# Two token tiles on four fixed experts instead of two experts at a time, with finer weight refills and a reordered last unit

## The chip, the cores and the metric

The kernel runs on one core of a Trainium2 chip. The metric is the device time of one execution in microseconds, lower is better; the core's span (first to last instruction) is inside it.

## What is computed

One transformer layer on 256 tokens of 1024 float32 values: a mixer (global and windowed attention, whose output projection is added to `h`), then a hierarchical mixture of experts, then a final RMSNorm. The part that matters here:

```
gl = xt @ w_group + b_group             # 4 groups, the best one is taken
el = xt @ w_expert + b_expert           # 8 experts per group, the best two are taken
h_e = silu(xt @ w_gate[e]) * (xt @ w_up[e])          # 1024 -> 512
y  += combine[:, e] * (h_e @ w_down[e])              # 512 -> 1024
out = rms_norm(h + y, final_g)
```

There are 32 experts of three 2 MB float32 matrices each, 201 MB in all, and every expert's weights are read from DRAM once.

## The kernel before

The 256 tokens are two tiles (`TT = 2`) of 128. Tokens of an expert are gathered into columns by a matmul with a 0/1 matrix (`pick`), run through gate, up and down, and scattered back to their rows by a matmul with the transposed weighted picks (`place_w`), summing in four PSUM banks Y0 to Y3.

**Units.** The 32 experts are worked in ten units (`WAYS`, line 45): a 2-way unit takes two experts of 64 columns, a 4-way unit four of 32. The columns of TensorE's array are split between them, so two matmuls of 64 columns, or four of 32, run side by side. Experts 0 to 3 are fixed in advance (units 0 and 1); the rest are sorted on the chip by token count, the four fullest of them in the 2-way units 4 and 5.

**Weights.** All weights go through a ring of 12 slots of 2 MB. Fill `f` of the ring (`fill_at`, unit, matrix, expert) is in slot `f % 12`. SyncE (SP) issues every load in order and waits, before each, until the last user of the slot is done (L345, and L374 to L389 for unit 2). The 12 slots take the four fixed experts before the routing is known; from there on a slot can be refilled only when (a) the order of the experts has been computed (`order_ready`, then `value_load` of each expert's number, L374) and (b) TensorE has done with what is in it. Unit 2's loads are the first that need both. Unit 2's gate matrices come in pieces as unit 0's gate product goes (`GATE_PIECES`, `load_chunks`, L389): 256 KB, 256 KB, then 512 KB each, for two experts; the rest of unit 2's 12 fills comes in halves of 1 MB (`load_piece`, L381).

**The order around the routing, written out by hand, per engine.** TensorE (PE): transposes `h` (`turn_h`, L1239), the last of the eight output projections (`project(0, 1, 1, 0)`, L1333), router logits of tile 0 and of tile 1 (`router_logits`, L1426), then rank and count matmuls (L1454 to L1466), gathers for unit 0 (`first_gather`, L1449), one matmul that turns the sort into expert numbers (L1593), and unit 0's gate product (L1584). VectorE (DVE): adds the projection (`add_projection`, L870), tile 0's routing chain (L976 to L1007: best group, best two experts, `chosen`), the same for tile 1, picks of unit 0 (`first_pick`, L1016), the sort (L1109 to L1122) interleaved with the combine weights (L1112 to L1138), the cast of the expert numbers (L1131), and the picks of the next units (L1068, L1077). ScalarE (ACT): squares for the second norm (L694, L701), copies of the transposes (L697, L703), gathered activations (L714), silu (L724), `y` copies (`copy_out`, L728).

**Steady state.** For each later unit: gather, transpose of the previous unit's activations (`turn_act`, L1525), down product (L1536), gate product (L1511), scatter (L1566), transposed picks (L1490), up product (L1511).

**The last unit.** Its down matrices arrive in five column pieces (`LAST_PIECES`, L449). After the up product PE runs the spread of the final gain over the partitions (`spread_final_g`, L1665, two halves, on either side of `turn_act`), the first half of down (`last_half`, L1536), then scatter and two quarters of down in turn (`last_quarter` L1684, `last_scatter` L1696), each scatter behind an ACT copy of what it scatters (`last_copy`, L738). ACT squares the sums (L745), DVE and GpSimd make the norm factor (L1220, L1212, L571), DVE and ACT scale, and the stores go out.

```
last_half(); last_scatter(0)
last_quarter(0, range(FC)); last_scatter(1)
last_quarter(1, ...);       last_scatter(2)
```

## Time and profile before

| | |
|---|---|
| three runs | 551.67 us median (551.37 to 551.74) |
| the profiled execution | 551.39 us |
| its span | 549.3 us |
| mean granted TensorE clock | 0.910 |
| TensorE busy | 445.6 us (81%) |
| VectorE, ScalarE, GpSimd busy | 108.3, 81.0, 28.4 us |
| SyncE's DMA queue | 214.89 MB, 94.2% of 16 engines' span |
| chain that ended last | PE 48%, DMA 47% of the span |

Times are microseconds from the first instruction. In the rows, PE is TensorE's matmul, PEld its weight load, DVE VectorE, ACT ScalarE, SPq SyncE's instructions that issue DMAs. L12 is line 12 of the kernel. "x4" is a count, and `[2.29 <-DMA ...]` the idle time of the engine just before, with what ended it.

### The profile page before, as it was taken

Reading aid. Unit: us, or ns where it says so; the run is one execution under the profiler, and the core shown is the slowest. Engines: PE = TensorE matmul, PEld = TensorE weight load, DVE = VectorE, ACT = ScalarE, POOL = GpSimd, SP = SyncE. Lnnn points to the kernel's source line nnn. Section 1 sums busy time; section 2 is a strip of 40 time slices with the busy share of each in tenths; the row PEclk is TensorE's granted clock in tenths of the full one; section 3 lists DMA queues with packets and bytes.
Section 4 is the critical chain, followed back from the end, with each engine's and each line's share of the span. In section 5 each row is a group of like instructions: output and inputs, shape, how many; then the busy total and the mean of one; then the engine's idle time right before and its main releaser. Section 6 shows DMA issues by size and latency. Waiting matters only on the chain.

```text
span 549.3 us, 6418 instructions
## 1 busy us (share of the span) xinstructions
PE 445.6 (81%) x2528; PEld 193.6 (35%) x2528; DVE 108.3 (20%) x352; ACT 81.0 (15%) x218; POOL 28.4 (5%) x61
## 2 busy tenths in 40 slices
PE   9999999999999985759999984863686295657794
PEld 4455554664453431323532521410223021312232
DVE  1028863251150300210200400400031000300012
ACT  1127653311100101000101001000100000000113
POOL 0242422100000000000000000000000000000000
PEclk9999999999999999779999988975878787977898
DMA  8989996959999999999999999999999999999992
GB/s 307 367 322 424 432 404 227 366 199 376 425 421 420 430 428 428 424 430 425 427 430 428 427 426 430 427 430 426 427 428 428 426 430 425 432 424 431 419 378 102
DMA packets 27822, 217.72 MB, mean 396 GB/s; under 512 B 5352, under 2 KB 7784, under 8 KB 14480
## 3 DMA queue, kind: packets, MB, share of 16 engines
q1 hardware_dynamic: 23552, 214.89, 94.2%
q10 hardware_dynamic: 4240, 2.42, 1.5%
q8 instruction: 21, 0.34, 0.3%
q14 instruction: 9, 0.07, 0.0%
HBM read 216.23 MB, written 1.06 MB: 396 GB/s over the span
## 4 chain that ended last, share of the span: by engine, by line
PE 48%; DMA 47%; another core or an unknown queue 1%; SPq 1%; issue 1%; DVE 1%; ACT 0%; DVEq 0%; POOL 0%
DMA ring<-in_w_up_dram 26%; DMA ring<-in_w_gate_dram 21%; PE bank L1511 18%; PE bank L1245 8%; PE bank L1333 5%; PE bank L1536 3%; PE bank L1287 2%; PE bank L1311 1%; PE bank L1299 1%; PE bank L1472 1%; PE bank L1566 1%; PE bank L1584 1%; SPq L345 1%; PE bank L1449 1%
## 5 line engine op out<-in xcount | busy, mean ns | idle before, releaser
L1511 PE MATMUL bank<-ring,head 128*32 128x512 f32 (+1 forms) x992 | 155.0, 676 | 69.3 <-DMA ring<-in_w_gate_dram 36.6
L1511 PEld LDWEIGHTS bank<-ring,head 128*32 128x32 f32 (+1 forms) x992 | 44.8, 128 | 170.1 <-issue 169.9
L1536 PE MATMUL bank<-ring,region_q 128*32 128x512 f32 (+1 forms) x480 | 75.8, 671 | 23.8 <-DMA ring<-in_w_down_dram 22.9
L1106 DVE COPY region_q<-bank 128x256 f32<-128x256 f32 x10 | 4.2, 424 | 300.8 <-PE bank L1490 300.8
L1536 PEld LDWEIGHTS bank<-ring,region_q 128*32 128x32 f32 (+1 forms) x480 | 22.3, 129 | 69.9 <-issue 69.3
L728 ACT ACTIVATE head<-bank 128x512 f32<-128x512 f32 x18 | 9.9, 595 | 234.7 <-PE bank L1566 228.1
L1245 PE MATMUL bank<-ring,head 128*128 128x512 f32 x96 | 44.4, 612 | 0.0
L1472 PEld LDWEIGHTS bank<-region_q,h 128*128 128x128 f32 x288 | 33.7, 192 | 8.2 <-issue 8.2
L1472 PE MATMUL bank<-region_q,h 128*128 128x128 f32 x288 | 36.3, 279 | 0.0
L1566 PE MATMUL bank<-head,region_q 128*128 128x512 f32 x72 | 33.3, 605 | 1.2 <-ACT head L728 1.2
L714 ACT ACTIVATE head<-bank,head 128x128 f32<-128x128 f32 x40 | 11.4, 369 | 121.4 <-PE bank L1472 119.9
L1245 PEld LDWEIGHTS bank<-ring,head 128*128 128x128 f32 x96 | 18.0, 196 | 21.4 <-issue 20.9
L571 POOL TENSOR_TENSOR stat<-stat 128x1 f32<-128x1 f32 x2 | 1.1, 550 | 434.7 <-DVE stat L1212 434.7
L1566 PEld LDWEIGHTS bank<-head,region_q 128*128 128x128 f32 x72 | 12.9, 189 | 21.6 <-issue 19.6
L1333 PE MATMUL bank<-ring,head 128*128 128x512 f32 x32 | 15.1, 598 | 0.0
L1333 PE MATMUL bank<-ring,region_q 128*128 128x512 f32 x32 | 14.7, 601 | 0.0
L1068 DVE TENSOR_SCALAR region_q<-cst,sorted_rw,stat 128x32 f32<-128x32 f32 (+1 forms) x56 | 12.4, 296 | 0.0
L1077 DVE TENSOR_SCALAR region_q<-cst,sorted_rw 128x32 f32<-128x32 f32 (+1 forms) x56 | 12.4, 295 | 0.0
L1095 DVE COPY region_q<-bank 128x512 f32<-128x512 f32 x10 | 6.9, 692 | 16.0 <-PE bank L1525 16.0
L1100 DVE TENSOR_TENSOR region_q<-region_q,bank 128x512 f32<-128x512 f32 x10 | 6.9, 687 | 16.1 <-PE bank L1511 16.1
L1090 DVE TENSOR_TENSOR head<-bank,head 128x512 f32<-128x512 f32 x9 | 6.2, 692 | 17.1 <-PE bank L1472 17.1
L870 DVE SCALAR_TENSOR_TENSOR h<-bank,stat,h 128x512 f32<-128x512 f32 x8 | 6.0, 751 | 16.4 <-PE bank L1333 9.8
(199 smaller groups left out, 310.9 us busy)
## 6 DMA issues: line engine op xcount, KB each, us to landing
ring<-in_w_gate_dram SPq DMA_DIRECT2D x28, 2048.0 KB, 39.5
ring<-in_w_up_dram SPq DMA_DIRECT2D x28, 2048.0 KB, 38.8
ring<-in_w_down_dram SPq DMA_DIRECT2D x24, 2048.0 KB, 39.2
ring<-in_w_down_dram SPq DMA_DIRECT2D x12, 1024.0 KB, 12.1
ring<-in_w_up_dram SPq DMA_DIRECT2D x8, 1024.0 KB, 10.0
ring<-in_w_o_dram SPq DMA_DIRECT2D x2, 2048.0 KB, 13.1
ring<-in_w_gate_dram SPq DMA_DIRECT2D x4, 1024.0 KB, 9.8
ring<-in_w_in_dram SPq DMA_DIRECT2D x7, 512.0 KB, 8.8
```

The source lines that it names most:

```text
L714: last = act.activation(xgT[:, c, :], ps[GD0 if i else FIRST_BANKS[c // 2]][:, c * P:(c + 1) * P], ACT.Copy, scale=g2_rows[:, c:c + 1])
L728: act.activation(y_slots[:, 512 * half:512 * half + 512], ps[(GD0 if i else Y0) + half][:], ACT.Copy).then_inc(y_ready, 1)
L1068: last = dve.tensor_scalar(pick[:, t, rows * a:rows * (a + 1)], iota1[:, 0:rows], ranks[:, t, e0 + a:e0 + a + 1], rstd2[:, t:t + 1], ALU.i ...
L1077: last = dve.tensor_scalar(pick_w[:, t, rows * a:rows * (a + 1)], iota1[:, 0:rows], ranks[:, t, e0 + a:e0 + a + 1], weights[:, t, e0 + a:e ...
L1095: dve.tensor_copy(hT, ps[GATE][:].rearrange("p (c s) -> p c s", c=FC)).then_inc(hT_ready, 1)
L1245: return pe.matmul(ps[bank][:], xT[:, c, t * P:(t + 1) * P], cols, start=(c == 0), stop=(c == KC - 1))
L1287: last = pe.matmul(ps[2 * (s % 2) + half][:, 256 * j:256 * j + 256], qkT[rows, 5 * g + 2 * jg + j, qt * P:(qt + 1) * P], qkT[rows, 5 * g + ...
L1333: last = pe.matmul(ps[bank][:], mixT[g][:, t, c, :], w_o_sb[g][:, c, 512 * half:512 * half + 512], start=(c == 0), stop=(c == 3))
L1472: last = pe.matmul(ps[GD0 + b][:, c * P:(c + 1) * P], h_cols[:, t, 4 * b + c, :], pick[:, t, :], start=(t == 0), stop=(t == TT - 1))
L1511: last = pe.matmul(ps[bank][rows, :], xgT[:, c, rows], slots[fill_slot(f + a)][:, c * F:(c + 1) * F], start=(c == 0), stop=(c == KC - 1))
L1536: last = pe.matmul(ps[bank + half][rows, :], hT[:, c, rows], down_cols(slots[fill_slot(f + a)], half, c), start=(c == 0), stop=(c == FC - 1))
L1566: last = pe.matmul(ps[Y0 + k][:], place_w[i % 2][:, (k // 2) * P:(k // 2 + 1) * P], y_slots[:, 512 * (k % 2):512 * (k % 2) + 512], start=( ...
```

## The change

Units 0 and 1 now hold one token tile each and both work with the same four fixed experts at 32 columns. The same 12 fills are loaded before the routing is known, and the same loads wait for the same steps of the attention (only the matrices that they carry differ). What changes:

- Tile 0 is picked, gathered and put through its first gate chunk before tile 1 has been routed. For that the last projection is split around tile 0's router logits, its addition on DVE is put into tile 0's routing chain, the squares for tile 1's norm are taken in two halves, and each tile has its own picks (`first_picks`, four instructions instead of two).
- The sort and the cast of the expert numbers stand ahead of the combine weights on DVE. On PE the expert-number matmul stands behind tile 0's whole gather and half of tile 1's.
- Each chunk of the fixed experts' weights is used for tile 0, then for tile 1, and is then free. Unit 2's gate matrices come in 16 loads of 256 KB and 8 of 512 KB, its up matrices in 8 of 512 KB and 4 of 1 MB, its down matrices in 8 of 1 MB.
- For a fixed expert the check on capacity uses the fuller of the two tiles against 32.
- `spread_final_g` moves ahead of the last unit's up product. The second quarter of the last down product follows the first without a scatter between, the scatter of the first quarter is split into its two tiles around the last chunk, and the last copy is made by DVE instead of ACT, before DVE's branch on the overflow flag. The final product of the first 512 columns is put ahead of that branch too.

```diff
-GATE_PIECES = ((0, 1), (1, 2), (2, 4), (4, 6), (6, 8))
+GATE_PIECES = ((0, 1), (1, 2), (2, 3), (3, 4), (4, 6), (6, 8))
+UP_PIECES = ((0, 2), (2, 4), (4, 8))
-WAYS = (2, 2, 4, 4, 2, 2, 4, 4, 4, 4)
+WAYS = (FIXED, FIXED, 4, 4, 2, 2, 4, 4, 4, 4)
...
SyncE, unit 2
             experts = order_of(2, range(2))
-            for k in range(PIECES):
...
+            for k, (lo, hi) in enumerate(GATE_PIECES):
+                if hi < KC:
                     sp.wait_ge(gate_pieces, k + 1)
                 else:
+                    sp.wait_ge(gate_done, 2)
+                for a in range(FIXED):
+                    if k == 0 and a >= 2:
+                        experts += order_of(2, range(a, a + 1))
+                    load_chunks(0, a, lo, hi, gate_pieces_in)
+            for k, (lo, hi) in enumerate(UP_PIECES):
...
+                for a in range(FIXED):
+                    load_chunks(1, a, lo, hi, up_pieces_in)
+            for half in range(2):
+                sp.wait_ge(down_done, 3 + half)
+                for a in range(FIXED):
+                    load_chunks(2, a, 4 * half, 4 * half + 4, down_half_in)
...
VectorE, routing
-            after(best_experts(0))
+            k_best = best_experts(0)
+            add_projection(0, 1, 1, 8, 0)
+            after(k_best)
             after(expert_places(0))
             link(two_hots(0))
             choose(0)
+            dve.wait_ge(chosen_ready, 1)
+            dve.tensor_copy(chosen_late[:, FIXED:EXPERTS], chosen[:, 0, FIXED:EXPERTS]).then_inc(chosen_ready, 1)
+            first_picks(0)
+            rank_tile(0)
...
-            dve.wait_ge(ranked, 2)
-            first_pick(1, 0)
-            first_pick(1, 1).then_inc(pick_ready, 1)
-            rank_tile(1)
+            first_picks(1)
+            k_rank = rank_tile(1)
...
TensorE, routing
             turn_h(0, 0)
             turn_h(0, 1)
-            project(0, 1, 1, 0)
-            turn_h(1, 0)
+            project(0, 1, 1, 0, range(0, 2))
             pe.wait_ge(hTr_act, 2)
             pe.wait_ge(router_ready, 1)
             router_logits(0, range(KC)).then_inc(routed, 1)
+            project(0, 1, 1, 0, range(2, 4))
+            turn_h(1, 0)
             turn_h(1, 1)
             pe.wait_ge(hTr_act, 3)
             router_logits(1, range(0, 4))
+            pe.wait_ge(chosen_ready, 1)
+            pe.matmul(ps[RANK0][:, 0:EXPERTS], upper_low, chosen[:, 0, :], start=True, stop=True).then_inc(ranked, 1)
             pe.wait_ge(hTr_act, 4)
             router_logits(1, range(4, 8)).then_inc(routed, 1)
...
+            pe.wait_ge(pick_ready, 1)
+            tile_gather(0, range(0, 4))
+            tile_gather(0, range(4, KC))
             pe.wait_ge(hots_ready, 1)
...
+            tile_products(0, 0, range(0, 1))
+            pe.wait_ge(pick_ready, 2)
+            tile_gather(1, range(0, 2))
+            tile_gather(1, range(2, 4))
+            pe.wait_ge(places_ready, 1)
+            pe.matmul(ps[ORDER][0:1, 128:128 + EXPERTS], expert_col, place_hot[0:EXPERTS], start=True, stop=True).then_inc(ordered, 1)
+            tile_products(1, 0, range(0, 1)).then_inc(gate_pieces, 1)
+            both_tiles(0, range(1, 2))
+            pe.wait_ge(xg_act, 1)
+            tile_gather(1, range(4, KC))
+            for lo, hi in GATE_PIECES[2:]:
+                both_tiles(0, range(lo, hi))
...
TensorE, last unit
                 if i == UNITS - 1:
                     scatter(i - 1)
+                    spread_final_g(0, GD0)
+                    spread_final_g(1, GD1)
...
-            spread_final_g(0, GD0)
             turn_act(UNITS - 1)
-            spread_final_g(1, UP)
...
             last_quarter(0, range(FC))
-            last_scatter(1)
             pe.wait_ge(last_in[2], 16 * 4)
-            pe.wait_ge(y_ready, 2 * (UNITS - 1) + 2)
             last_quarter(1, range(0, 2))
             pe.wait_ge(last_in[3], 16 * 4)
             last_quarter(1, range(2, 3))
+            last_scatter(1, range(0, 1))
             pe.wait_ge(last_in[4], 16 * 4)
             last_quarter(1, range(3, 4))
+            last_scatter(1, range(1, 2))
             last_scatter(2)
```

The new helpers: `tile_gather(t, chunks)` is one 128x128 matmul per chunk of tile `t`; `tile_products(t, m, chunks)` is four matmuls of 32 columns per chunk; `both_tiles` runs it for tile 0, then tile 1, and signals SyncE; `tile_down(t)` is `down` for one tile.

## Rows read from the trace of the kernel before

**Rows 1.** The page's slices: GB/s in 40 equal slices of the span.
```profile
GB/s 307 367 322 424 432 404 227 366 199 376 425 421 420 430 428 428 424 430 425 427 430 428 427 426 430 427 430 426 427 428 428 426 430 425 432 424 431 419 378 102
```

**Rows 2.** Windows: from:to and length, busy by engine, clock, DMA share, GB/s.
```profile
170.00:530.00 360.00, 266.63 (x1658) 102.54 (x1658) 39.06 (x127) 21.47 (x54) 0.00 (x0) 0.87 1.01 427
117.00:142.00 25.00, 25.00 (x138) 11.54 (x134) 4.01 (x12) 3.03 (x8) 0.00 (x0) 1.00 0.95 353
117.00:118.00 1.00, 1.00 (x8) 0.42 (x6) 0.00 (x0) 0.10 (x1) 0.00 (x0) 1.00 0.02 6
118.00:122.00 4.00, 4.00 (x24) 2.04 (x22) 2.03 (x8) 0.00 (x0) 0.00 (x0) 1.00 0.90 262
122.00:126.00 4.00, 4.00 (x22) 1.38 (x20) 0.60 (x3) 0.60 (x1) 0.00 (x0) 1.00 1.01 377
```

**Rows 3.** SyncE's waits from 100 to 180 us: total, times, longest.
```profile
SPq L374 <- DVE stat L1133: 9.7, 1, 9.7
```

**Rows 4.** Timeline, the routing up to the first refill: start, duration, instruction.
```profile
102.02 3.60 PE L1333 MATMUL bank<-ring,region_q 128*128 128x512 f32 x8
105.66 0.75 DVE L870 SCALAR_TENSOR_TENSOR h<-bank,stat,h 128x512 f32<-128x512 f32 x1 [3.56 <-PE bank L1333]
105.89 1.95 PE L1426 MATMUL bank<-region_q,head 128*128 128x128 f32 x16
107.98 0.22 DVE L976 SCALAR_TENSOR_TENSOR region_q<-bank,stat,router_b 128x4 f32<-128x4 f32 x1 [1.55 <-PE bank L1426]
...
109.98 0.19 DVE L1007 TENSOR_TENSOR region_q<-region_q 128x32 f32<-128x32 f32 x1
...
113.46 1.60 PE L1449 MATMUL bank<-region_q,h 128*128 128x128 f32 x12
...
114.99 0.21 PE L1593 MATMUL bank<-stat,cst 32*1 32x32 f32 x2
115.24 0.18 DVE L1131 CAST expert_at<-bank 1x32 int32<-1x32 f32 x1 [0.15 <-PE bank L1593]
116.96 0.36 SPq L389 DMA_DIRECT2D ring<-in_w_gate_dram  x1
```

**Rows 5.** Timeline, a later set of 32-column picks on VectorE.
```profile
152.06 1.75 DVE L1068 TENSOR_SCALAR region_q<-cst,sorted_rw,stat 128x32 f32<-128x32 f32 x8
```

**Rows 6.** DMA issues by size (us from issue to landing), four issues in a row, expert-number loads.
```profile
ring<-in_w_gate_dram SPq DMA_DIRECT2D x4, 256.0 KB, 3.4
```
```profile
178.42 1.89 SPq L345 DMA_DIRECT2D ring<-in_w_gate_dram  x4
```
```profile
L374 SPq TENSOR_LOAD <-expert_at x28: 260/266/468, 115.5 to 436.9; - x28
```

**Rows 7.** Timeline of TensorE from the last up product on.
```profile
517.90 5.34 PE L1511 MATMUL bank<-ring,head 128*32 128x512 f32 x32 [2.29 <-DMA ring<-in_w_up_dram]
...
523.53 3.64 PE L1511 MATMUL bank<-ring,head 128*32 128x512 f32 x32
527.10 1.16 PE L1665 MATMUL bank<-cst,head 128*128 128x128 f32 x8
...
535.90 1.93 PE L1684 MATMUL bank<-ring,region_q 128*32 128x256 f32 x32
538.34 1.13 PE L1696 MATMUL bank<-head,region_q 128*128 128x256 f32 x4 [0.50 <-ACT head L738]
...
541.83 1.13 PE L1696 MATMUL bank<-head,region_q 128*128 128x256 f32 x4 [0.50 <-ACT head L738]
```

**Rows 8.** TensorE's waits from 480 us on: total, times, longest.
```profile
PE bank L1511 <- DMA ring<-in_w_up_dram: 2.3, 1, 2.3
PE bank L1696 <- ACT head L738: 1.7, 3, 0.7
PE bank L1566 <- ACT head L728: 1.2, 1, 1.2
```

**Rows 9.** Windows around the last up product: columns as in rows 2.
```profile
516.00:518.00 2.00, 0.10 (x4) 0.13 (x8) 0.00 (x0) 0.00 (x0) 0.00 (x0) 1.00 1.00 418
520.00:522.00 2.00, 2.00 (x12) 0.54 (x8) 0.00 (x0) 0.00 (x0) 0.00 (x0) 0.50 1.03 422
```

More of the change, by code:

```diff
@@ L1499, in landed, with products @@
                 pe.wait_ge(slot_in[fill_slot(f)], 16 * fill_count(f))
-            def products(i, n_e, f, bank, done, pieces=None, every=2, picks=False, chunks=range(KC)):
+            def products(i, n_e, f, bank, done, picks=False):
                 pe.wait_ge(xg_act, i + 1)
@@ L1564, in scatter @@
                 pe.wait_ge(place_ready, i + 1)
-                for k in range(4):
-                    last = pe.matmul(ps[Y0 + k][:], place_w[i % 2][:, (k // 2) * P:(k // 2 + 1) * P],
-                                     y_slots[:, 512 * (k % 2):512 * (k % 2) + 512], start=(i == 0), stop=False)
-                    last.then_inc(scattered, 1)
+                for t in tiles(i):
+                    for half in range(2):
+                        last = pe.matmul(ps[Y0 + 2 * t + half][:], place_w[i % 2][:, t * P:(t + 1) * P],
+                                         y_slots[:, 512 * half:512 * half + 512], start=(i < ONE_TILE), stop=False)
+                        last.then_inc(scattered, TT // len(tiles(i)))
                 return last
@@ L1744, in _ @@
                             for c in range(FC):
[L1745 removed]
+                                last = pe.matmul(ps[3 + half][:], hT[:, c, :], down_cols(slots[OVER_SLOT + 2], half, c),
                                                  start=(c == 0), stop=(c == FC - 1))
```

536 lines of the change are left out of this document (248 added, 288 removed).

## The prediction, made before the changed kernel was run

> **What bounds the kernel now.** I read the slices first: the core moves 420 to 432 GB/s in nearly every slice from 137 us (slice 11) to 508 us, and falls to 199 to 376 GB/s in slices 7 to 10 [rows 1]. The windows then put numbers on it: 427 GB/s and a DMA share of 1.01 from 170 to 530 us, while TensorE is busy for 267 of those 360 us [rows 2]. So in this stretch the weight stream is the bound and TensorE has slack. 32 experts of weights must pass whatever the order of work, and the change keeps their bytes. It can gain or lose at two places only: when and how fast the stream restarts behind the routing, and how long the chain is from the last up weights to the end.
>
> The restart: SyncE sits 9.7 us in one wait, for DVE's order of the experts [rows 3]. The chain behind it is PE's expert-number matmul at 114.99, the cast at 115.24, the first refill at 116.96 [rows 4]. The end: PE waits 2.29 us for the last up weights until 517.90, then works without a DMA wait to the last scatter at 541.83 [rows 7, 8].
>
> The sum is made against the profiled execution, 551.39 us with a span of 549.3; the median of the runs stands 0.28 us above it.
>
> **Part 1, TensorE's work on the fixed experts.** Before: two units of 24 chunk groups, two matmuls side by side in each. After: two tiles of 24 groups, four side by side. Thirty-two matmuls of that form (8 groups) took 3.64 us [rows 7], 0.455 us a group, so 48 groups are about 22 us either way. Scatters and gathers of the two units halve. Price zero: the cover is the stream, which needs 25 MB / 427 GB/s, some 59 us, for the 12 slots that this work frees. All 16.8 MB of gate and up fills are freed by about 138 us by this count, the down slots some 10 us later, and the stream reaches them only at 118.7 + 16.8 MB / 0.427 = 158 us. If the cover were gone, a late `turn_act` (DVE makes unit 2's picks before the product of tile 0, about 4 us) would be paid.
>
> **Part 2, when the order is known.** I move each step in the timeline.
> - Tile 0. Half the projection (1.80 of 3.60 us), then the logits (1.95) [rows 4]: logits done at 105.8, 2.1 us earlier than now. DVE's chain starts at 105.9. `add_projection` now stands inside it and waits for the projection's second half (to 107.5); it takes 0.75, so the chain's 2.19 us (from L976 at 107.98 to the end of L1007 at 110.17) [rows 4] becomes 3.2: `chosen` at 109.1, 1.1 us earlier.
> - Tile 1. `h` is complete at 108.3 instead of 106.4. Transposes, ACT's copy behind the second half of the square, and eight chunks of logits with the rank matmul between end at 111.2 instead of 110.1. DVE meanwhile makes four picks of tile 0; eight of them take 1.75 us, so 0.22 each [rows 5], 0.9 in all, then the rank. Its second chain starts at 111.4 and gives the two hots at 113.4, about 1 us later than now.
> - PE is behind by then: tile 0's whole gather is 16 instructions. Twelve take 1.60 us [rows 4], so 2.1 us, from 111.8 to 113.9. Then the ranks, DVE's four picks of tile 1 (0.9) at 114.6 to 115.5, its rank, the sort (0.9, ending 116.4). On PE half of tile 1's gather (1.1) runs beside it, to 116.7.
> - So the expert-number matmul stands at about 116.7, not 114.99: **+1.7 us**. The load of the numbers and the first issue follow as now. Tile 1's first gate chunk is done by about 117.5, before SyncE needs it at 118.7. The last fixed fill (down, 2 MB) is issued 1.9 us later with `projected`, at 107.5, and ends near 114.6, still before the restart. Bounds of this term: +0.4 (DVE's picks and PE's gather all hidden, only the 1 us of tile 1 minus what the sort gains by standing alone) to +3.0 (my chain plus one more round trip between the engines at each of the five handovers).
>
> **Part 3, how fast the stream fills after the restart.** Before: 353 GB/s from 117 to 142 is 8.8 MB, which at 427 takes 20.7 us, so 4.3 us are lost here. Nearly 1 us of it is the start (6 GB/s from 117 to 118), then 262 GB/s while the 256 KB pieces run, 377 while 512 KB ones do [rows 2]. After: 16 pieces of 256 KB instead of 4. SyncE issues one each 0.52 us (four issues in 1.89, less 0.33 for the last, by three) [rows 6], except in the first round, where a number is loaded ahead of the third and fourth, 0.27 us for the load instruction alone [rows 6] and about 0.55 with its checks. A 256 KB piece moves in 0.61 us at 427 GB/s, so after the first four the queue gets deep, as it never was before. I take 0.95 us for the start, 262 GB/s for the first MB (4.0 us), and 350 GB/s for the other 3.1 MB, between the 377 of the half-MB pieces and the 262: 9.0 us. That is 13.9 us for 4.2 MB, against 9.8 at full rate, 4.1 lost. The 16 loads of 512 KB (8.4 MB) are taken close to the full rate with a deep queue, 0.3 lost. Sum 4.4 against 4.3: **+0.1 us**. Bounds: -2.1 (start, and 377 GB/s for all of the 4.2 MB) and +5.4 (262 for the 4.2 MB, 6.2 lost, and 377 for the 8.4 MB, 2.6 lost, with the start 9.7 to 9.8).
>
> A rule speaks against this step. The Trainium skill, "DMA: Bandwidth & Descriptors", section Bandwidth, says to batch transfers to 1 MiB or more for 75% of peak, and lists 341 GB/s for 1 MB alone. The trace half agrees: four 256 KB pieces ran at 262 GB/s; but half-MB ones in a queue ran at 377, above that table's 1 MB.
>
> **Part 4, the last unit.** The scatters wait for ACT's copies three times, 1.7 us in all, the first 0.7, the other two 0.5 each [rows 8]. Both 0.5 go: the first quarter's copy runs beside the second quarter (1.93) and the last copy, now on DVE, beside half a scatter (0.57 of 1.13) [rows 7]. Two scatter halves lengthened by a wait for the square of tile 1 give about 0.15 back: **-0.85 us**. DVE's branch on the flag moves to before the norm factor; I cost it at nothing, covered by the last scatter and squares. Bounds -1.0 to 0 (branch and copy not covered, or the last weights land too late: they must land by about 539).
>
> The spread (1.16 + about 1.1 us) [rows 7] was hidden beside DVE's product and copy; moving it away saves nothing there. But it now fills the 2.29 us in which PE waits for the up weights. The window 516:518 shows PE busy for 0.10 of 2 us at full clock, then 520:522 shows the clock granted at 0.50, the 1.2 GHz level [rows 9], and the first half of the up product takes 5.34 us where the second takes 3.64 [rows 7]. With the spread in that gap I expect full clock: **-1.7 us**, bounds -1.7 and 0.
>
> **The sum:** 551.39 + 1.7 + 0.1 - 0.85 - 1.7 = 550.64, plus 0.28 for the median: 550.9 us. About 0.2% (1.1 us) is what a measurement of this kernel can tell from no change, so the likeliest case counts as the same, close to its edge.
>
> **Rivals.**
> - *The clock falls all the same.* PE still has the 1.2 us wait for ACT's `y` copies before the last scatter of the steady state [rows 8]. Then 552.6, at the upper edge of no change. For it: the granted clock averages 0.87 from 170 to 530 us [rows 2], so it falls often. Against: the gap is nearly gone. Chance 0.22, split about evenly between same and slower.
> - *Small refills run slowly.* Place: SyncE's queue from 118.7 us on. Price +5.4 instead of +0.1: 556.2. It decides from the point where the first 4.2 MB run below about 280 GB/s (15.9 us with the start instead of 13.9), which brings the sum over 552.8. For it: 262 GB/s is the only measured rate of 256 KB pieces. Against: in that window only four such pieces were to be had, with SyncE waiting for TensorE. Chance 0.12, slower.
> - *The order is known no later.* If the sort without interleaved work and tile 0's early start make up for the picks, the +1.7 is 0.4 or less: 549.6, faster. For it: tile 0 is 1.1 us earlier. Against: the order needs tile 1, and tile 1's `h` comes 1.9 us later. Chance 0.22.
> - *The change does nothing measurable.* Restart as now, tail bound by the last weights: 551.7. Chance 0.06.
>
> The forecast has the remaining 0.38, its own range 549.8 to 552.2, of which 0.12 lie below 550.6. So faster 0.12 + 0.22 = 0.34, slower 0.11 + 0.12 = 0.23 and with the forecast's far end 0.25, same 0.41. The range that leaves out 2 in 10: 549.2 (under it the case of an early restart with a fast refill, 0.1) to 554.0 (above it the slow refills, 0.1).
>
> **What would show it.** The expert-number matmul near 116.7 and the first refill near 118.7 (part 2); a window of 25 us from the first refill on at about 350 GB/s (part 3); from 170 us on 427 GB/s as now (part 1; if PE's late work starved the stream, the rate would dip between 140 and 165 us); the last up product in about 7.4 us instead of 9.2, and one ACT wait before L1696's successors instead of three (part 4). I am wrong if the first refill starts before 117.5 or after 120, or if the last up product's first half keeps 5.3 us.

## The result, and the profile of the changed kernel

The changed kernel takes **553.74 us** (median of 7 runs) beside 551.37 for the kernel before on the same chip (7 runs, 549.65 to 552.3): ratio **1.0047**, 95% interval [1.0031, 1.0063], so 1.7 to 3.5 us slower. The forecast was 550.9. One execution of the changed kernel took 1478.22 us; no run of this study explains it, and the interval leaves it out (the median of the other six is 553.51). The profiled execution took 552.5 us, its span is 550.6.

The page's slices, in GB/s of 40 equal slices, answer to [rows 1]:

```profile
GB/s 317 359 329 426 429 405 233 315 202 354 404 387 420 429 427 427 427 430 427 426 430 423 432 424 430 425 431 426 428 427 427 428 427 427 427 427 430 420 405 150
```

Slices 10 to 13 are what to look at (slice 1 is the first). The kernel before reached 425 in slice 11 and kept it; here it is 404, then 387, and 420 only from slice 13 on. The windows (columns as in [rows 2]) put the loss into stretches. First the changed kernel, then two stretches of the kernel before that were not shown yet:

```profile
117.00:142.00 25.00, 25.00 (x228) 8.86 (x224) 6.49 (x31) 1.97 (x3) 0.00 (x0) 1.00 0.91 315
118.00:120.00 2.00, 2.00 (x20) 1.13 (x16) 0.19 (x1) 0.00 (x0) 0.00 (x0) 1.00 0.57 150
120.00:124.00 4.00, 4.00 (x44) 1.22 (x40) 2.56 (x12) 0.00 (x0) 0.00 (x0) 1.00 0.88 262
124.00:128.00 4.00, 4.00 (x44) 1.25 (x40) 0.00 (x0) 0.00 (x0) 0.00 (x0) 1.00 0.94 262
160.00:168.00 8.00, 8.00 (x80) 2.85 (x73) 0.00 (x0) 0.00 (x0) 0.00 (x0) 1.00 0.91 356
170.00:530.00 360.00, 258.01 (x1606) 99.59 (x1598) 38.36 (x126) 21.78 (x54) 0.00 (x0) 0.86 1.01 427
```
```profile
118.00:142.00 24.00, 24.00 (x132) 11.11 (x128) 4.01 (x12) 2.94 (x7) 0.00 (x0) 1.00 0.99 367
160.00:168.00 8.00, 7.12 (x47) 4.67 (x48) 1.38 (x2) 1.14 (x4) 0.00 (x0) 1.00 1.02 422
```

From 170 us on both run at 427 GB/s, so a byte that is late at 170 stays late. The yardstick of this study is therefore the **loss** of a stretch: its length times (1 - rate / 427). From 118 to 142 us it is 3.4 us before and 5.6 after, from 142 to 160 it is 0.2 and 0.5, from 160 to 168 it is 0.1 and 1.3. The sum is 3.7 us before and 7.4 after, **3.7 us more**. The last up weights show the same: they let TensorE start at 521.31 instead of 517.90.

SyncE's waits (100 to 180 us; total, times, longest), answering to [rows 3], name who holds the refills back, and the timeline answers to [rows 4] for the restart:

```profile
SPq L395 <- PE bank L1559: 15.1, 2, 13.8
SPq L395 <- PE bank L1532: 9.4, 3, 6.7
SPq L389 <- DVE stat L1123: 9.1, 1, 9.1
```
```profile
101.42 1.88 PE L1335 MATMUL bank<-ring,region_q 128*128 128x512 f32 x4
105.22 0.22 DVE L975 SCALAR_TENSOR_TENSOR region_q<-bank,stat,router_b 128x4 f32<-128x4 f32 x1 [3.57 <-PE bank L1428]
108.06 0.19 DVE L1006 TENSOR_TENSOR region_q<-region_q 128x32 f32<-128x32 f32 x1
110.44 0.22 DVE L975 SCALAR_TENSOR_TENSOR region_q<-bank,stat,router_b 128x4 f32<-128x4 f32 x1
113.18 0.94 DVE L1017 TENSOR_SCALAR region_q<-cst,bank,stat 128x32 f32<-128x32 f32 x4 [0.40 <-PE bank L1463]
115.69 0.21 PE L1630 MATMUL bank<-stat,cst 32*1 32x32 f32 x2
116.01 0.18 DVE L1122 CAST expert_at<-bank 1x32 int32<-1x32 f32 x1 [0.88 <-PE bank L1630]
117.71 0.36 SPq L395 DMA_DIRECT2D ring<-in_w_gate_dram  x1
```

The first refill is at 117.71 instead of 116.96, but this execution reached the last projection 0.6 us earlier (101.42, first line, against 102.02 in [rows 4]). Counted from the start of that projection the first refill stands at 14.94 us in all six profiles that keep the code before up to there. It stands at 16.29 to 16.31 in nine of the eleven with the changed routing, and at 15.88 in a_order_first and a_both, which move the expert-number matmul forward. So the changed kernel's first refill comes **1.35 us later**.

Counted in the same way, the loss is 4.3 us more, the 3.7 of above and the 0.6 by which this execution was ahead. It can be read from windows of 51 us that begin 15 us behind the start of that projection. Before, then after:

```profile
117.02:168.02 51.00, 50.12 (x275) 23.52 (x273) 13.17 (x45) 5.34 (x14) 0.00 (x0) 1.00 0.98 388
116.42:167.42 51.00, 49.88 (x452) 19.70 (x444) 12.41 (x50) 5.47 (x11) 0.00 (x0) 1.00 0.94 352
```

That is 4.7 us lost against 9.0. These 51 us hold the later start, the slower restart and the dry stretch together, and a profile gives them more surely than a part of them: 386 to 389 GB/s in the six profiles that keep the code before, 351 to 355 in the nine of the changed kernel and its variants that leave no work out.

Next, TensorE's work on the fixed experts, and SyncE at the down refills:

```profile
139.21 5.36 PE L1532 MATMUL bank<-ring,head 128*32 128x512 f32 x48
147.23 7.05 PE L1559 MATMUL bank<-ring,region_q 128*32 128x512 f32 x64
154.21 2.05 PE L1472 MATMUL bank<-region_q,h 128*128 128x128 f32 x16
159.40 7.07 PE L1559 MATMUL bank<-ring,region_q 128*32 128x512 f32 x64 [0.88 <-DVE head L1084]
```
```profile
163.09 5.22 SPq L395 DMA_DIRECT2D ring<-in_w_down_dram  x8
```

The second down product runs from 159.4, and only its halves free the down slots. SyncE waits 13.8 us for that; the stream is dry before 163, and this is the 1.3 us of 160:168. It sets a floor, too. The first down refill is issued 61.7 us behind the start of the projection, and until then only the 16.8 MB of gate and up refills can move. At 427 GB/s they take 39.3 of the 46.7 us that the window of 51 us has up to there. At least 7.4 us are lost by then, however good the restart is. The tail, answering to [rows 7 to 9]:

```profile
521.31 3.64 PE L1516 MATMUL bank<-ring,head 128*32 128x512 f32 x32 [0.42 <-DMA ring<-in_w_up_dram]
525.25 3.64 PE L1516 MATMUL bank<-ring,head 128*32 128x512 f32 x32
537.58 3.48 PE L1686 MATMUL bank<-ring,region_q 128*32 128x256 f32 x56
540.99 0.70 PE L1698 MATMUL bank<-head,region_q 128*128 128x256 f32 x2
541.67 0.64 PE L1686 MATMUL bank<-ring,region_q 128*32 128x256 f32 x8
542.24 1.96 PE L1698 MATMUL bank<-head,region_q 128*128 128x256 f32 x6
```
```profile
PE bank L1698 <- ACT head L738: 0.7, 1, 0.7
```
```profile
520.00:522.00 2.00, 1.58 (x17) 1.04 (x19) 0.00 (x0) 1.19 (x2) 0.00 (x0) 1.00 0.98 410
```

The up product runs at the 2.4 GHz level, both halves in 3.64 us. From the start of the first quarter to the end of the last scatter it is 6.62 us against 7.06 (535.90 to 542.96) before. This tail is 2.1 us shorter than the one of the profile before (from the start of the up product to the end of the span 29.3 us, against 31.4).

### The profile page after: what moved, and what is told of

It reads as the page before. It is cut to its first block, busy times and chain, and to the rows that moved or that the text cites. A ratio compares the mean times of both kernels' runs of the same rounds, so it can differ in the third digit from the quotient of the medians.

```text
span 550.6 us, 6764 instructions
## 1 busy us (share of the span) xinstructions
PE 437.0 (79%) x2676; PEld 186.0 (34%) x2676; DVE 108.1 (20%) x355; ACT 81.5 (15%) x223; POOL 28.6 (5%) x62
## 4 chain that ended last, share of the span: by engine, by line
PE 48%; DMA 41%; SPq 8%; DVE 1%; issue 1%; DVEq 0%; POOL 0%; ACT 0%
DMA ring<-in_w_down_dram 27%; DMA ring<-in_w_gate_dram 13%; PE bank L1559 10%; PE bank L1516 8%; PE bank L1247 7%; SPq L432 7%; PE bank L1335 5%; PE bank L1532 4%; PE bank L1472 2%; PE bank L1289 2%; PE bank L1313 1%; PE bank L1301 1%; PE bank L1590 1%; PE bank L1598 1%; DMA ring<-in_w_in_dram 1%
## 5 line engine op out<-in xcount | busy, mean ns | idle before, releaser
L1516 PE MATMUL bank<-ring,head 128*32 128x512 f32 (+1 forms) x896 | 135.1, 694 | 77.5 <-DMA ring<-in_w_gate_dram 47.7
L1516 PEld LDWEIGHTS bank<-ring,head 128*32 128x32 f32 (+1 forms) x896 | 38.8, 129 | 166.6 <-issue 166.6
L1472 PEld LDWEIGHTS bank<-region_q,h 128*128 128x128 f32 x256 | 29.9, 192 | 6.7 <-issue 6.7
L1472 PE MATMUL bank<-region_q,h 128*128 128x128 f32 x256 | 32.0, 278 | 0.0
L1590 PE MATMUL bank<-head,region_q 128*128 128x512 f32 x64 | 29.9, 607 | 1.2 <-ACT head L728 1.2
L1532 PE MATMUL bank<-ring,head 128*32 128x512 f32 x256 | 28.7, 594 | 0.0
L717 ACT ACTIVATE head<-bank,head 128x128 f32<-128x128 f32 x32 | 9.1, 368 | 102.4 <-PE bank L1472 102.4
L1590 PEld LDWEIGHTS bank<-head,region_q 128*128 128x128 f32 x64 | 11.4, 189 | 19.7 <-issue 17.7
L1335 PE MATMUL bank<-ring,head 128*128 128x512 f32 x32 | 15.1, 598 | 0.0
L1532 PEld LDWEIGHTS bank<-ring,head 128*32 128x32 f32 x256 | 7.7, 110 | 16.1 <-issue 15.5
L1289 PE MATMUL bank<-ring 64*128 64x256 f32 x64 | 8.8, 398 | 0.5 <-issue 0.5
## 6 DMA issues: line engine op xcount, KB each, us to landing
ring<-in_w_down_dram SPq DMA_DIRECT2D x12, 1024.0 KB, 15.9
ring<-in_w_up_dram SPq DMA_DIRECT2D x8, 512.0 KB, 13.9
```

Of the source, the lines that this page charges most:

```text
L1289: last = pe.matmul(ps[2 * (s % 2) + half][:, 256 * j:256 * j + 256], qkT[rows, 5 * g + 2 * jg + j, qt * P:(qt + 1) * P], qkT[rows, 5 * g + ...
L1335: last = pe.matmul(ps[bank][:], mixT[g][:, t, c, :], w_o_sb[g][:, c, 512 * half:512 * half + 512], start=(c == 0), stop=(c == 3))
L1472: last = pe.matmul(ps[GD0 + b][:, c * P:(c + 1) * P], h_cols[:, t, 4 * b + c, :], pick[:, t, :], start=(t == 0), stop=(t == TT - 1))
L1516: last = pe.matmul(ps[bank][rows, :], xgT[:, c, rows], slots[fill_slot(f + a)][:, c * F:(c + 1) * F], start=(c == 0), stop=(c == KC - 1))
L1532: last = pe.matmul(ps[(GATES, UPS)[m][t]][rows, :], xg_tile[t][:, c, rows], slots[fill_slot(fill_at(t, m, a))][:, c * F:(c + 1) * F], star ...
L1590: last = pe.matmul(ps[Y0 + 2 * t + half][:], place_w[i % 2][:, t * P:(t + 1) * P], y_slots[:, 512 * half:512 * half + 512], start=(i < ONE ...
```

## The experiments

Eighteen kernels were run, all but one timed beside the kernel before on the same chip (medians of it 550.1 to 550.7). Ratios are to that kernel. Losses are from windows of one profile each. From 118 to 142 us two profiles of the same code up to there differ by 0.4 us (before and b_spread, 3.4 and 3.8) and by as much as 1.1 (the changed kernel and a_down, 5.6 and 6.7), so a difference of 1 us in that stretch alone says little.

### First the tail: b_spread, b_tail, b_order

b_spread is the kernel before with the spread moved as in the change, b_tail adds the reordered last scatters, b_order has those alone.

```
+                    spread_final_g(0, GD0)
+                    spread_final_g(1, GD1)
-            spread_final_g(0, GD0)
             turn_act(UNITS - 1)
-            spread_final_g(1, UP)
```

> The kernel before with one part of the change alone: the spread of the final gain stands ahead of the last up product (and the output's slots are those of the changed kernel). Main account: the changed kernel's trace has the first half of the last up product at 3.64 us instead of 5.34, so 1.7 us come from the clock that no longer falls; this kernel should be 1.7 us under the kernel before, about 549.7. Rival: the clock stayed up because of something else (the weights came 3.4 us later there); then the first half keeps 5.3 us here and the time stays at 551.4.

> The kernel before with the whole reordered last unit and nothing else of the change. Main account: 1.7 us from the clock and 0.4 us from the order of the last scatters (the trace of the changed kernel has 6.6 us from the first quarter to the last scatter's end, before 7.06), so 549.3. Rival, the prediction's term: 0.85 us from the order, 548.8. Rival that the last unit gives nothing: 551.4.

> The kernel before with the reordered last scatters alone: own banks for the three last pieces, the last copy on DVE, the half-scatters between the quarters. The spread of the final gain stays behind the last up product. Theory (the tail's gain of 0.44 us in the changed kernel is real and independent of the rest): 0.3 to 0.6 us under before. Rival (the last down weights land too late for it, or DVE's copy takes it back): within 0.2 us of before.

Measured: b_spread 550.42, ratio 0.9994 [0.9978, 1.0010]. b_tail 549.73, 0.9993 [0.9976, 1.0010]. b_order 550.44, 1.0007 [0.9994, 1.0021]. None can be told from no change. The tail of b_order in the trace of TensorE:

```profile
518.49 3.64 PE L1516 MATMUL bank<-ring,head 128*32 128x512 f32 x32 [1.60 <-DMA ring<-in_w_up_dram]
534.80 3.29 PE L1689 MATMUL bank<-ring,region_q 128*32 128x256 f32 x56
539.36 1.96 PE L1701 MATMUL bank<-head,region_q 128*128 128x256 f32 x6
```

Two things are to be seen. The scatters' gain is there (534.80 to 541.32 is 6.52 us instead of 7.06) but the measured time does not show it. And the up product runs at full clock **without** the spread in front of it. The same product without the spread before it is in b_pieces (a wait of 1.46 us for the weights, 3.64), b_late (1.39, 3.64), a_spread_back (1.94, 3.64), b_late_pieces (2.39, 5.34), b_rows (2.19, 5.34) and the kernel before (2.29, 5.34). So the slow half came after the three longest waits only, and the wait is that long in some executions. In b_tail, where the up product ran at 3.64 behind the spread, the fall came a product later:

```profile
528.34 5.34 PE L1541 MATMUL bank<-ring,region_q 128*32 128x512 f32 x32 [0.78 <-DVE region_q L1095]
```

a_coarse and a_refill show the same 5.34 in that place, nine other kernels with the same two waits ahead of it (0.88 and 0.78 us) do not. What the spread takes from one product is not safely won.

### Small changes to the changed kernel: a_cap64, a_order_first, a_coarse, a_down, a_both

a_cap64 restores the fixed experts' limit of 64 tokens in the capacity flag alone. a_order_first puts the expert-number matmul ahead of half of tile 1's first gathers. a_coarse has the gate pieces of before (8 of 256 KB, 12 of 512). a_down frees the down slots after two chunks. a_both joins a_down and a_order_first.

```
 c[FIXED:EXPERTS, C_WIDE_COL] = HALF_CAP           # a_cap64: c[0:EXPERTS, ...]
             tile_gather(1, range(0, 2))
-            tile_gather(1, range(2, 4))
             pe.wait_ge(places_ready, 1)
             pe.matmul(ps[ORDER]...).then_inc(ordered, 1)
+            tile_gather(1, range(2, 4))
-GATE_PIECES = ((0, 1), (1, 2), (2, 3), (3, 4), (4, 6), (6, 8))
+GATE_PIECES = ((0, 1), (1, 2), (2, 4), (4, 6), (6, 8))
+                        if t and half == 0 and c == 1:
+                            last.then_inc(down_pieces, 1)
```

> The changed kernel with the capacity check of the fixed experts at 64 per tile instead of 32; left out is the treatment of a fixed expert's tokens beyond 32 in one tile, everything else is the same. Main account: the one execution of the changed kernel at 1478 us took the overflow branch, because in that draw of the inputs a fixed expert has more than 32 tokens in one tile; with this check no execution is near 1478, and the others are as in the changed kernel, 553 to 554. Rival: the long execution was a disturbance, and it can come or not in any kernel.

> The changed kernel with the expert-number matmul after a quarter of tile 1's gather instead of after half of it. Main account: the matmul moves from 115.69 to about 115.15, the first refill from 117.71 to 117.15, and as the stream is the bound the kernel gains 0.5 us. Rival: the stream is later held up by the release of the down slots at 163 us anyway, so what the restart gains is lost there, and the time stays within 0.1 us.

> The changed kernel with its gate pieces cut as in the kernel before (chunks 2 and 3 in one load): 8 loads of 256 KB and 12 of 512 KB. Account 'small loads': half of the 256 KB pieces go, the stretch from 124 to 130 us runs at 350 to 377 GB/s instead of 262, and the kernel gains 0.6 to 1 us. Account 'release': the pieces of chunks 2 and 3 are released 1.8 us later for the first of them, and the kernel stays or loses 0.3 us.

> The changed kernel with the first half of unit 2's down matrices in two loads each, the first of which starts when the second chunk of tile 1's down product is done instead of the fourth. In the changed kernel's trace the stream runs dry from 162 to 166 us, 1.3 us of it lost, because that release comes at 163 us. Account 'TensorE is late': the release moves 1.8 us forward, the stream doesn't run dry, the window from 142 to 170 goes from 400 to about 418 GB/s and the kernel gains 1.2 us. Account 'small loads' alone: the window stays near 400 and the time at 553.5.

> The changed kernel with two refill repairs at once: the expert-number matmul ahead of half of tile 1's first gathers, and the down slots of tile 1 freed after two chunks of the first half. Theory (each mended a part of the stream's loss that the other left): 552.6 to 553.2. Rival (what is won at one place is lost at the next, since the loss of 118 to 132 us has another cause): 553.2 to 553.8 as with either alone.

Measured: a_cap64 553.39, ratio 1.0054 [1.0029, 1.0078]; a_order_first 553.59, 1.0056 [1.0036, 1.0075]; a_coarse 553.38, 1.0048 [1.0033, 1.0064]; a_down 553.45, 1.0047 [1.0033, 1.0061]; a_both 553.4, 1.0054 [1.0039, 1.0068]. None gives back anything that can be measured. Their losses from 118 to 142 and from 160 to 168 us: 5.9 and 1.3, 6.2 and 1.4, 5.5 and 2.0, 6.7 and 0.3, 6.0 and 1.4. So a_down's profile has no dry stretch, but it had lost more before it, and its edit touches nothing that runs there; a_both has the same edit and both losses as before. Over the 51 us all five are alike: 353, 351, 352, 353 and 355 GB/s, 8.6 to 9.1 us lost, where the changed kernel loses 9.0. What one place gains the other takes back. That is the rival of a_order_first, and it fits the floor of 7.4 us: whatever is won at the restart, the stream waits for the down slots afterwards. The floor is not all of it: a_down and a_both have the first down refill at 60.0 and 60.1 us instead of 61.7, which lowers it to 5.7 and 5.9, and they lose as much.

### The branch for overflowing experts: a_over

In the changed kernel a fixed expert holds 32 tokens of a tile before the flag is raised, where it held 64 before. a_over forces the flag, to see whether the one execution of 1478 us took that branch.

> The changed kernel with the overflow flag set always, so that every engine takes the branch that loads all 32 experts again; no token is above the capacity, so the branch adds nothing to the sum. If the one execution of the changed kernel at 1478 us took that branch, this takes about 1478 us, with a granted clock of 1.0. If it takes clearly more or less, that execution was something else.

Measured, in one execution: 2962.51 us, clock 0.835. The execution at 1478 us had a clock of 1.0 and half the time, so it was not this branch as a whole. It did not come again in a_cap64, nor in any kernel that keeps the limit of 32, so a_cap64 decides nothing about it. Its cause stays open.

### What each cause is worth on the kernel before: b_pieces, b_late, b_late_pieces

```
+GATE_PIECES = ((0, 1), (1, 2), ..., (7, 8))       # b_pieces: 16 pieces of 256 KB
             pe.wait_ge(places_ready, 1)           # b_late
+            first_gate(range(0, 2))
             pe.matmul(ps[ORDER]...).then_inc(ordered, 1)
-            first_gate(range(0, 4))
+            first_gate(range(2, 4))
```

> The kernel before with unit 2's first two gate matrices in 16 loads of 256 KB instead of 4 of 256 KB and 6 of 512 KB; nothing else. Account 'small loads': the 256 KB pieces run at 262 GB/s whatever the order of the work, so the 25 us from 117 to 142 move about 0.4 MB less than 353 GB/s x 25 us and the kernel loses about 1 us. Account 'release': the stream behind the restart is held by when TensorE frees the slots, and the pieces cost nothing; then the window stays at 345 to 353 GB/s and the time within 0.3 us.

> The kernel before, with the expert-number matmul moved behind the first two chunk groups of unit 0's gate product (1.8 us of TensorE work by the profile of before, where a group is two pairs of records). It prices the later order by itself. Theory (the stream is the bound, so what the restart loses reaches the end, and TensorE's freed slots give back only little): first refill about 119 instead of 117, 552.0 to 552.8 us, ratio 1.0025 to 1.004. Rival (the refills come faster after a late restart since more chunks are free by then, so the end hardly moves): within 0.5 us of before.

> The kernel before with both of the changed kernel's restart properties: the expert-number matmul behind two chunk groups (as in b_late) and 16 gate refills of 256 KB (as in b_pieces). Theory (the causes add up: later order 2.6 us by b_late's median, small rows 0.2 by b_pieces): 552.6 to 553.6, loss of the stream between 118 and 142 us about 5 us, as in the changed kernel. Rival (a later restart leaves more chunks free, so the small pieces cost nothing on top): as b_late, below 552.8 with a loss under 4.6.

Measured: b_pieces 550.82, ratio 1.0003 [0.9987, 1.0019]. b_late 552.84, **1.005** [1.0035, 1.0065]. b_late_pieces 552.43, 1.0041 [1.0024, 1.0058]. The window 118:142 of b_late:

```profile
118.00:142.00 24.00, 24.00 (x133) 11.05 (x128) 4.13 (x13) 2.93 (x7) 0.00 (x0) 1.00 0.93 348
```

The loss there is 4.4 us, 1.1 more than before. Counted from the start of the projection its first refill stands at 16.97 us, 2.03 later than before's, and the windows of 51 us are, for b_late and then b_late_pieces:

```profile
116.79:167.79 51.00, 50.12 (x276) 23.65 (x276) 14.18 (x52) 5.32 (x14) 0.00 (x0) 1.00 0.95 377
117.21:168.21 51.00, 50.12 (x276) 23.64 (x276) 14.20 (x52) 5.34 (x14) 0.00 (x0) 1.00 0.95 368
```

So in the stream the delay of 2.0 us costs 1.3 us, and with the small pieces 2.4, though these alone cost 0.1 (b_pieces has 387 GB/s). By the times the delay costs 1.9 to 3.6 us. The two do not agree, and the profiled execution of b_late was its fastest. Shown is that a later restart costs something; whether free chunks make up a part of it, as the rival has it, stays open. In b_late_pieces the stream loses more and the time is no worse than b_late's. And b_late alone is as slow against the kernel before as the whole change (1.005 and 1.0047), so times can't say how the 2.4 us are shared out.

### Rows of 2 and 4 KB in a full queue: b_rows

```
+BITS = (1, 1, 1, 1, 1, 8, 1, 4, 1, 1)
+for k in range(BITS[u]):
+    cols = slice(k * SLOT // BITS[u], (k + 1) * SLOT // BITS[u])
+    sp.dma_start(slots[s][:, cols], ...).then_inc(slot_in[s], 16)
```

> The kernel before, with the weights of unit 5 (12.6 MB) loaded in pieces of 256 KB, so that each partition's row is 2 KB, and those of unit 7 (25.2 MB) in pieces of 512 KB with rows of 4 KB, both deep in a full queue and far from the restart. It measures the piece size by itself. Theory (rows of 2 and 4 KB move slower even with work queued: after's trace has 2048-byte packets at 91 to 116 ns and 4096-byte ones at about 165 ns, where 8192-byte ones take 313): 300 to 360 GB/s in unit 5's stretch and about 390 in unit 7's, 8 to 14 us more in all. Rival (the low rates behind the restart come from the shallow queue alone): 427 GB/s in both stretches and the time of before, within 1 us.

Measured: 555.94 us, ratio 1.0097 [1.0071, 1.0124]. The windows hold unit 5's pieces of 256 KB, unit 7's of 512 KB, and whole slots:

```profile
280.00:300.00 20.00, 19.07 (x58) 6.04 (x56) 0.00 (x0) 1.58 (x3) 0.00 (x0) 1.00 1.05 387
370.00:410.00 40.00, 20.27 (x132) 5.87 (x124) 0.00 (x0) 1.57 (x3) 0.00 (x0) 0.79 1.03 409
440.00:480.00 40.00, 27.31 (x174) 10.87 (x174) 5.74 (x20) 2.72 (x7) 0.00 (x0) 0.80 1.01 427
```

387, 409 and 427 GB/s: the size costs something with a full DMA share, but less than the theory took from the restart's rates (5.3 us in the time by the ratio, where it gave 8 to 14). Over the 4.2 MB of 256 KB pieces and 8.4 MB of 512 KB ones that the changed kernel has, that makes 1.0 and 0.9 us, and before it had 1.0 MB and 3.1 MB, 0.2 and 0.3. Net **1.3 us** at b_rows' rates, which the pieces behind the restart did not reach. In the Trainium skill, "DMA: Bandwidth & Descriptors", section Bandwidth asks for 1 MiB and more for 75% of peak; by this run 256 KB already gets 91% of the full rate when the queue is full.

### Who holds the restart: a_skip, a_up_wide, a_refill, a_lean, a_spread_back

a_skip leaves out chunks 1 to 6 of tile 1's gate and up products (about 11 us of TensorE work). a_up_wide loads the up refills in halves. a_refill has a lean order: two known experts' first and second chunks, then the other two numbers and 512 KB pieces, 18 gate pieces instead of 24, and a_up_wide's halves. a_lean is a_skip and a_refill together. a_spread_back returns the spread to its old place.

```
+                    if t == 1 and 0 < c < KC - 1:        # a_skip
+                        continue
+UP_PIECES = ((0, 4), (4, 8))                             # a_up_wide
-                for a in range(FIXED):                   # a_refill
-                    if k == 0 and a >= 2:
-                        experts += order_of(2, range(a, a + 1))
+                for a in range(FIXED if k else 2):
+                    if k == 1 and a == 2:
+                        experts += order_of(2, range(2, 4))
+                    load_chunks(0, a, 0 if k == 1 and a >= 2 else lo, hi, gate_pieces_in)
```

> The changed kernel, with six of the eight chunk groups of tile 1's gate and of its up product left out (chunks 1 to 6), so that its outputs for the fixed experts are not the reference's. TensorE has 12 groups of 0.91 us less to do, some 11 us, and frees the gate, up and down slots sooner; the order is known as late as in the changed kernel. Theory (TensorE's work between 118 and 166 us keeps the stream waiting): the dry stretch at 160 to 168 and most of the loss between 120 and 132 us go, 551.0 to 552.0. Rival (the later order and the pace at which SyncE issues do it): the stream loses as much between 118 and 132 as in the changed kernel, and the time stays at 552.8 to 553.6.

> The changed kernel with its up refills in halves of 1 MB (rows of 8 KB) instead of two quarters and a half; the first half waits for four chunks instead of two. Theory (a row of 4 KB moves at about 390 GB/s, one of 8 KB at 418, which makes about 0.7 us over the 4.2 MB that change size): 0.3 to 0.9 us under the changed kernel, 552.5 to 553.1. Rival (the later first half leaves the queue empty for as long): no gain, 553.2 to 553.9.

> The changed kernel with a leaner refill order for unit 2: in the first round two pieces of 256 KB only, for the two experts whose numbers are known, then their second chunks, then the other two numbers and two pieces of 512 KB, then quarters of 512 KB; the up refills in halves as in the run beside it. 18 gate pieces instead of 24, 4 of 256 KB instead of 16, and no number is loaded within the first round. Theory (the loss from 118 to 142 us is SyncE's issue rate and the small rows): the loss there falls from 5.6 us to about 4, the time to 551.8 to 552.8. Rival (TensorE frees the chunks no faster than they are loaded): 553.0 to 553.9.

> The changed kernel with the lean refill order of a_refill and with chunks 1 to 6 of tile 1's gate and up products left out as in a_skip, so that its outputs for the fixed experts are not the reference's. Theory (what remains is the later order alone): dry stretch at 160 to 168 gone, loss from 118 to 142 us about 4.5, 551.8 to 552.6, near b_late's 552.8. Rival (four experts' refills restart slower than two experts' whatever their size): loss above 5.2 in that stretch and 552.6 to 553.2.

> The changed kernel with the spread of the final gain back behind the last up product and behind turn_act, as before. Theory (the stream decides when the last up weights land, the spread lies in a wait for them): within 0.5 us of the changed kernel, 553.0 to 553.9. Rival (the gate product of the last unit runs so long, at the lower clock, that the spread of 1.95 us stands on the path to the up product): 0.5 to 1.5 us less, 552.2 to 553.0.

Measured: a_skip 552.84, ratio 1.0047 [1.0033, 1.0062]; a_up_wide 553.62, 1.0059 [1.0039, 1.0078]; a_refill 553.2, 1.0049 [1.003, 1.0068]; **a_lean 551.79, 1.0018** [1.0003, 1.0032]; a_spread_back 553.27, 1.0058 [1.0043, 1.0074]. The windows of a_skip, then of a_lean:

```profile
118.00:142.00 24.00, 22.04 (x196) 8.15 (x196) 10.00 (x41) 1.94 (x4) 0.00 (x0) 1.00 0.93 318
160.00:168.00 8.00, 8.00 (x64) 2.67 (x60) 0.00 (x0) 0.92 (x2) 0.00 (x0) 1.00 1.01 421
```
```profile
118.00:142.00 24.00, 22.04 (x196) 8.17 (x196) 10.18 (x42) 2.15 (x4) 0.00 (x0) 1.00 0.92 338
160.00:168.00 8.00, 8.00 (x64) 2.68 (x60) 0.00 (x0) 0.71 (x2) 0.00 (x0) 1.00 1.01 419
```

a_skip has TensorE out of the way: SyncE's waits for the fixed experts' products between 116 and 172 us fall from 24.5 us in five waits to 9.1 in two. The dry stretch is gone, and the restart loses 6.1 us all the same. SyncE's pace is not what holds it there either: by 130 us it had issued 17 pieces, 4.7 MB, and 2.8 MB had moved. a_refill has fewer and larger pieces, and SyncE waits for TensorE the longer, five times for the gate and up products (116 to 172 us):

```profile
SPq L395 <- PE bank L1532: 17.1, 5, 7.9
SPq L395 <- PE bank L1559: 15.1, 2, 13.8
```

It loses 5.4 and then 2.0. Either alone leaves the ratio where the changed kernel has it (1.0047 and 1.0049); both together bring it to 1.0018, 1.6 us less, with an interval that ends just below that of a_skip. a_skip missed its theory (551.0 to 552.0); a_lean's time held its own, with 5.0 us lost at the restart instead of 4.5. By medians a_lean is 1.0 us under a_skip and 1.4 under a_refill. The windows of 51 us of a_refill, a_skip and a_lean say it more finely:

```profile
116.81:167.81 51.00, 49.89 (x452) 19.69 (x444) 12.41 (x50) 5.46 (x11) 0.00 (x0) 1.00 0.93 353
116.79:167.79 51.00, 48.17 (x420) 19.32 (x412) 12.42 (x50) 6.18 (x13) 0.00 (x0) 1.00 0.96 360
117.00:168.00 51.00, 48.17 (x420) 19.34 (x412) 12.43 (x50) 6.19 (x13) 0.00 (x0) 1.00 0.95 373
```

Lost are 8.8, 8.0 and 6.4 us, against 9.0 in the changed kernel: the refill order alone gives about 0.1, TensorE's work alone 1.0, both 2.5. So the stream has **two limits one behind the other**, the time at which TensorE frees the four down slots, which a_skip brings forward by 8.6 us (the first down refill stands at 53.1 us instead of 61.7), and the slow restart with many small refills, and the first hides the second. Whether the size of the pieces, their number or their order makes the restart better in a_lean is not shown; a_up_wide (1.0059) and a_coarse (1.0048) alone gave nothing, with TensorE's limit in place. a_lean still loses 1.8 us more than before in the stream (0.2 to 1.8 us in the time), with its first refill 1.4 us later; that the later order is the cause of it is not shown by itself. a_spread_back has the time of the changed kernel, so there the place of the spread is worth nothing that can be measured. No kernel of the study is measurably faster than the one before.

## Why the prediction was wrong, point by point

**What bounds the kernel** held: 427 GB/s from 170 us on in every kernel but b_rows, which was made to be slower there, and whatever the stream lost before that reached the end. The two places were the right ones. A third, TensorE's work on the fixed experts, had been put aside.

**Part 1 failed** ("price zero ... 0.455 us a group, so 48 groups are about 22 us"). In these rows a matmul has two records: a product of four experts over eight chunks is x64, not x32. Thirty-two records are four groups, one takes 0.91 us and 48 take 44. The cover was then read with that error: "all gate and up fills are freed by about 138 us, the down slots some 10 us later" against a stream that arrives at 158. The up slots were free at 147, the down slots from 163. The sum of work is indeed the same in both kernels, but its order is not. Before, unit 0 goes through gate, up and down and gives six slots back before unit 1 gives any; after, all four experts' down slots come last. That is the dry stretch, 1.2 us more than before, and the floor of 7.4 us over the 51 us, of which before loses 4.7: at least 2.7 of the 4.3 us that the stream lost more follow from this step alone, however the restart had gone. Taking TensorE's work away gives 1.0 us with the refills as they are (a_skip) and 2.4 with the lean ones (a_lean against a_refill, 8.8 to 6.4).

**Part 2** ("+1.7 us", bounds +0.4 to +3.0) had the right mechanism: tile 0 came earlier, tile 1's chain and picks later. It measures +1.35, within its bounds. b_late's delay of 2.0 us costs 1.3 us in the stream and 1.9 to 3.6 in the time, so what the term does to the time is not known better than that. The rival "the order is known no later" is out: 0.4 was its limit.

**Part 3** ("+0.1 us", bounds -2.1 to +5.4) was mis-sized. The 25 us from the first refill on ran at 326 GB/s (117.71:142.71), where about 350 was forecast and before has 352 (116.96:141.96): 5.9 us lost against 4.4, so **+1.5 us instead of +0.1**. The first 4.2 MB had moved 15.1 us after the first refill, by the packet records of the trace, against 13.9 forecast. The rate of 262 was rightly read as that of the small pieces at a restart, but it also held from 124 to 128, where the queue was expected to be deep. The rival "small refills run slowly" had the sign and about a quarter of its price of 5.4, and stayed short of the 15.9 us from which it was to decide. It is not shown to be the size alone: the small pieces cost the stream 0.1 us in b_pieces and 1.1 on top of b_late's delay, and a_refill shows that with fewer of them TensorE is the limit.

**Part 4** ("-0.85" and "-1.7 us"). The scatters gave 0.44 up to the end of the last one (0.54 in b_order), since the last ones still wait a little for the square and the copy, and 0.66 up to the start of the last scaling on DVE (544.99 and 543.97, counted from the first quarter). In b_order none of it shows in the time. The clock's 1.7 us stood in the one profile of before, and the changed kernel's profile has it, but four of the seven kernels with the spread in its old place ran the product at full clock as well. The term that failed is that of a stall in one execution booked as one of the median.

**The sum** in the profiles: +4.3 from the stream, -2.1 from the tail is 2.2; the spans, counted from the start of the last projection, differ by 1.9 (449.2 and 447.3 us). The medians differ by 2.4. How much of the tail's gain is in them can't be told: b_tail has between 1.3 us less and 0.5 more. The forecast of a gain failed by the stream, +4.3 where parts 1 to 3 had +1.8: at least 2.7 by the floor, which part 1 had put at nothing. The later order (1.35) and the slower restart (1.5) come to about as much together; without them the floor would still have cost its 2.7. That the measured 553.74 lies inside the stated range of 549.2 to 554.0 is luck: its upper part was there for a clock that falls and for slow refills, not for TensorE's work.

## What to carry to other kernels

When a stream is the bound, cost a reorder by when each buffer comes free, in the order in which the stream asks for them: the same TensorE work, done four experts abreast, frees the last third of the buffers at one late point. Count records against matmuls before dividing a duration by them. Where a stream meets two limits one behind the other, mending the first shows nothing while the second stands: mend both, as in the run that gave 1.6 us where each alone gave nothing that the times could show. And count a short delay from an event just ahead of it in the same execution: from the start of the profile the first refill scattered by 0.9 us in one and the same code, from the start of the projection by less than 0.02.

## What the runs showed that had not been expected

- The DMA rate stays low for some 12 us after the restart even with work queued. In a_refill 4 MB had been issued by 125.5 us and 1.8 MB moved, yet by the packet records of the trace 4096-byte packets took 246 to 284 ns on average from 127 to 130 us and 159 ns from 132 on. In the kernel before the 8192-byte ones took 880 ns at 130 and 310 from 132 on. Why is open.
- With a full queue the rate in b_rows is 387 GB/s for rows of 2 KB, 409 for 4 KB and 427 for 16 KB.
- The granted clock fell to the 1.2 GHz level in the up product after waits of 2.19, 2.29 and 2.39 us and after none of 0.21 to 1.94 us. In the down product behind two waits of 0.88 and 0.78 it fell in three of twelve kernels. What those three have in common is open.
